# Who makes the lower weight parts in the recurrence stage: VectorE or GpSimd

## What is computed

```
q, k, v, xr, yr = split(rms_norm(x) @ w_in)
attn_out = attention(q, k, v)
xc = depthwise_conv(xr)                       # 4 taps
r, i = sigmoid(xc @ wa + ba), sigmoid(xc @ wx + bx)
a = exp(8 * r * log_sigmoid(lam));  b = sqrt(1 - a*a) * i * xc
h_t = a_t * h_(t-1) + b_t                     # forward, and once more backward
lru_out = (h_fwd + h_bwd) * gelu(yr)
x = x + concat(attn_out, lru_out) @ w_out     # the first output projection
```

## Time and profile before

| | us |
|---|---|
| median of 3 runs (3453.57 to 3456.44) | 3454.61 |
| the profiled execution, its own time | 3458.81 |
| its span in the trace | 3457.0 |
| TensorE busy in the span | 3363.4 (97%) |
| VectorE, ScalarE, GpSimd busy | 2208.1, 1435.4, 1123.1 |

### The profile page before, as it was taken

The page is one execution under the profiler, slowest core; times in us unless marked ns, Lnnn a source line. Parts: engine busy times, 40 slices in busy tenths (PEclk is TensorE's granted clock), DMA queues, the critical chain, the costliest instruction groups (busy, mean ns, idle before and its releaser), DMA issues.

```text
span 3457.0 us, 44808 instructions
## 1 busy us (share of the span) xinstructions
PE 3363.4 (97%) x16634; PEld 2711.7 (78%) x16634; DVE 2208.1 (64%) x2247; ACT 1435.4 (42%) x1901; POOL 1123.1 (32%) x644
## 2 busy tenths in 40 slices
PE   9999899999999999999999999999889999999998
PEld 6677777888888868888887777777667878888886
DVE  8996968777773474322277888888856564444434
ACT  5688835444441142333223443344453353333213
POOL 2000028888832212111111111111112376766222
PEclk9999999999999999999999999999999999999999
DMA  4210221222252112111111110111122212223322
GB/s 143 62 44 19 73 90 67 81 85 79 85 195 95 48 43 92 36 42 36 37 49 43 37 42 31 42 42 36 43 79 85 79 63 90 76 88 122 134 89 82
DMA packets 59167, 242.52 MB, mean 70 GB/s; under 512 B 6592, under 2 KB 6592, under 8 KB 53312
## 3 DMA queue, kind: packets, MB, share of 16 engines
q1 hardware_dynamic: 59072, 241.22, 19.7%
HBM read 194.53 MB, written 41.42 MB: 68 GB/s over the span
## 4 chain that ended last, share of the span: by engine, by line
PE 81%; DVE 13%; issue 3%; ACT 3%; DMA 0%; POOL 0%; DVEq 0%; POOLq 0%; ACTq 0%
PE ps L508 45%; PE ps L1459 24%; PE ps L2699 2%; PE ps L2711 2%; PE ps L2688 1%; PE ps L2849 1%; PE ps L2862 1%; DVE conv_acc L2312 1%; DVE t_wide L1096 1%; PE ps L531 1%; PE ps L2801 1%; PE ps L2856 1%; PE ps L2835 1%; DVE small L2352 1%; PE ps L2797 1%
## 5 line engine op out<-in xcount | busy, mean ns | idle before, releaser
L479 POOL TENSOR_TENSOR w_lo_part<-w_raw,w_hi_part 128x1024 fp32r<-128x1024 f32 x162 | 404.7, 2498 | 1736.3 <-ACT w_hi_part L462 1736.3
L508 PE MATMUL ps<-h_hi_part,w_hi_part 128*128 128x512 f32 x1904 | 623.5, 408 | 30.1 <-DVE h_lo_part L1632 12.0
L508 PE MATMUL ps<-h_lo_part,w_hi_part 128*128 128x512 f32 x1904 | 594.7, 393 | 0.0
L508 PE MATMUL ps<-h_hi_part,w_lo_part 128*128 128x512 f32 x1904 | 593.1, 392 | 0.0
L462 ACT ACTIVATE w_hi_part<-w_raw 128x1024 fp32r<-128x1024 f32 x180 | 189.1, 1051 | 719.5 <-PE ps L508 631.7
L508 PEld LDWEIGHTS ps<-h_hi_part,w_hi_part 128*128 128x128 f32 x1904 | 346.4, 190 | 126.0 <-issue 41.6
L508 PEld LDWEIGHTS ps<-h_hi_part,w_lo_part 128*128 128x128 f32 x1904 | 360.5, 189 | 78.2
L508 PEld LDWEIGHTS ps<-h_lo_part,w_hi_part 128*128 128x128 f32 x1904 | 360.6, 189 | 78.0 <-issue 0.3
L2312 DVE SCALAR_TENSOR_TENSOR conv_acc<-u_pad,cols,conv_acc 128x1024 f32<-128x1024 f32 x232 | 307.3, 1325 | 19.4 <-DVE conv_acc L2312 2.7
L2151 DVE TENSOR_TENSOR residual<-residual,ps 128x1024 f32<-128x1024 f32 (+1 forms) x60 | 73.2, 1220 | 268.0 <-PE ps L508 267.9
L508 PE MATMUL ps<-u_hi,w_hi_part 128*128 128x512 f32 x736 | 232.0, 390 | 0.0
(11 more groups left out here) (449 smaller groups left out, 6596.8 us busy)
## 6 DMA issues: line engine op xcount, KB each, us to landing
w_raw<-in_w SPq DMA_DIRECT2D x226, 512.0 KB, 3.3
w_raw_odd<-in_w SPq DMA_DIRECT2D x46, 512.0 KB, 3.8
u_spill<-ffn_u SPq DMA_DIRECT2D x46, 512.0 KB, 3.0
u_wide<-u_spill SPq DMA_DIRECT2D x23, 1024.0 KB, 9.1
residual<-in_x SPq DMA_DIRECT2D x4, 1024.0 KB, 10.5
both_halves<-q_chan SPq DMA_DIRECT2D x16, 256.0 KB, 4.4
x_again<-in_x SPq DMA_DIRECT2D x8, 512.0 KB, 3.9
residual<-in_x SPq DMA_DIRECT2D x2, 2048.0 KB, 7.2
```

What stands on the lines that cost most here:

```text
L479: pool.tensor_tensor(WLO[:, slot], WRAW[:, slot], f32(WHI[:, slot]), ALU.subtract).then_inc(w_ready, 1)
L508: last = pe.matmul(PS[:, ps, b * HALF:(b + 1) * HALF], st[:, slot, k, :], at(mv, k, b), start=(k == 0 and n == 0), stop=(k == nk - 1 and n ...
```

## The change

The lower parts of jobs 9 to 19 are made by GpSimd, in the order of the jobs, each as soon as its upper part is there. VectorE no longer makes them; of this stage only job 20's stays with it. The arithmetic is the same.

```diff
@@ gpsimd_program
             splits_pool(pool, 0, J_GATE[0] + 1)
-            split_rest(pool, J_GATE[0] + 1)
+            for j in range(J_GATE[0] + 1, J_OUT + 2):
+                split_rest(pool, j)
             pool.wait_ge(w_ready, J_OUT + 2)
@@ vector_program
             def conv(t):
-                split_rest(dve, J_GATE[t])
                 dve.wait_ge(xc_tap, t + 1)
...
                 st.do(dve.tensor_tensor_scan(y[:, way], p[:, way], i[:, way], 0.0, ALU.mult, ALU.add))
-                if d == 0:
-                    split_rest(dve, J_YR[t] + 2)
-
-            dve.wait_ge(w_ready, J_GATE[0] + 2)
+
             for t in range(4):
                 inputs(t)
-                split_rest(dve, J_GATE[t] + 2)
                 if t < 3:
                     conv(t + 1)
```

## The result

The changed kernel takes 3462.37 us (median of 21 runs, 3460.01 to 3465.94), the kernel before, in as many runs beside it, 3458.41. The ratio is 1.0014, with a 95% interval of 1.0008 to 1.0020: the change makes the kernel slower, by 4.0 us or 0.11% by the medians. The profiled execution took 3464.93 with a span of 3462.8; that of before, 3458.81 and 3457.0.

The account below looks back on a forecast made before the run. VectorE's row from first tap to last product was taken as the bound: 112.0 less 12.1 removed plus 16.4 of holds gives 116.3, +4.3 us, so 3454.61 + 4.3 = 3458.9 us; 8-in-10 range 3454 to 3463.

Parts of the forecast that it names:

- VectorE's row as the bound: First tap (326.18) to last product (end 438.15): VectorE's nearly unbroken work, 112.0 us, sets when everything behind starts.
- What is removed, 12.1: VectorE's stretch: nine subtractions of jobs 11 to 19 and three gaps go, 12.1 us, leaving 99.9 of 112.0.
- the three gaps: VectorE's waits of 1.17 ahead of job 14, 1.14 ahead of a scan, 0.41 ahead of taps; counted as gone.
- The hold, 7 x 2.08 + 2 x 0.9 = 16.4: GpSimd's subtractions delay VectorE's two-operand instructions: seven full tiles at 2.08, two halves at 0.9, 16.4 us added.
- the row at 452.43: VectorE instruction with one PSUM operand, 1.21 with GpSimd at work from 452.74; taken to show PSUM readers are not held.
- No hold: Rival: VectorE's plain f32 instructions run beside GpSimd; TensorE's pace limits the gain to -5.8, 3448.8 us; chance 0.05.
- Little change: Rival: GpSimd begins ahead of VectorE's instruction in gaps left, 1.06 per full tile; -2.9, 3451.7 us; chance 0.08.
- Full hold: Rival: GpSimd blocks VectorE for its whole printed instruction, 2.41 full, 1.2 half; +7.2, 3461.8 us; chance 0.17.
- what the sum means: +4.3 us (0.12%) set against 0.2%, 6.9 us, as what a measurement can tell; 0.81 on within it.
- The absolute time: Median forecast for the changed kernel: 3454.61 + 4.3 = 3458.9 us.
- Whatever moves the end moves everything behind it by the same amount: Behind VectorE's last product: residual load, clearing, addition and TensorE's next job at 448.03 all shift equally, 4.3 us later.

Follow-up runs that it names:

- the spare reads: Kernel before, plus eleven unneeded 128x512 subtractions on GpSimd, VectorE still making the lower parts: 3465.98 against 3457.49, ratio 1.0027.
- writes alone: Kernel before, plus eleven GpSimd memsets of 128x512 at the same upper parts, no operand read: 3458.37 against 3457.49, ratio 1.0003.
- version with the halves beside the taps: Changed kernel, GpSimd's half tiles of jobs 13 and 16 also waiting for inputs(t) to end: 3463.51 against 3457.49, again 3461.87 against 3458.27.
- the version that removed them without GpSimd: Kernel before, VectorE making jobs 12, 15 and 18 ahead of inputs(t): 3455.62 against 3457.49, again 3456.86 against 3458.27.
- the version with GpSimd only where it costs nothing: Changed kernel, GpSimd keeping jobs 8, 9, 10, 13, 16, last two beside taps; VectorE makes 12, 15, 18 early: 3454.20 against 3458.27, again 3454.66 against 3458.37.

## Why the prediction was right and where it was wrong

**VectorE's row as the bound: right.** The stretch follows VectorE's instructions, holds and gaps in the changed kernel and the six others, and each came out within 0.5 us of its expectation but for the spare reads (2.6 off). The medians go with it as far as they can tell, with intervals of 2 to 4 us to either side: stretches of 108.1, 109.1, 111.8, 112.0 (writes alone), 116.2 and 120.6 have times of -4.1 (again -3.7), -1.9 (again -1.4), +0.9, +0.9, +4.0 (again +4.4) and +8.5 us against before. The version with the halves beside the taps (114.2; +6.0 and +3.6) is the one that doesn't fit. From the end of the stretch to TensorE's next start, 9.8 to 10.3 us pass in every kernel, so the link to that start holds as well.

**What is removed, 12.1: right.** The nine subtractions are gone and so are the three gaps. That the gaps were late weights and not something else is shown by the version that removed them without GpSimd.

**The hold, 7 x 2.08 + 2 x 0.9 = 16.4: right.** Measured on the full tiles: L2511 3.24, 3.22 and 3.23 (2.01 more on the mean), the scans 4.38, 4.37 and 4.37 (2.08 more), L2523 3.20 (1.97 more); on the halves 3.46 - 2.48 = 0.98 twice. The sum is 3 x 2.01 + 3 x 2.08 + 1.97 + 2 x 0.98 = 16.2. They stand where the prediction put them, but for job 19, of which it named the direction alone. 112.0 - 12.1 + 16.2 = 116.1, and 116.2 was measured. Two small things were off without a part in the sum: GpSimd's rows are printed up to 4.20 long, not 3.4, and the row at 452.43 could not show that an instruction that reads PSUM is free, since VectorE had begun it before GpSimd; the taps beside the moved halves show it (3.92).

**The rivals.** *No hold* fell by these rows and by the spare reads. *Little change*, where GpSimd begins first and costs 1.06, fell too: VectorE has no idle time in the row, so GpSimd never began first. At 344.98 it waited 0.43 for L2523's end, was printed 2.70, and the scan paid in full. *Full hold* fell by its size: GpSimd's printed 2.4 hold VectorE for 2.0 to 2.1. The sentence of the Trainium skill on which it stood (SBUF — State Buffer, section "Who interferes with whom") is right that the two exclude each other; the runs here show 0.3 to 0.4 us less of it than the 2.41 that GpSimd's undisturbed row prints. The price goes by GpSimd's tile and not by VectorE's instruction: one that takes 1.22 and a scan of 2.29 pay the same 2.0 to 2.1.

**The step that failed: what the sum means.** Every case of mine of any weight had a sign, and the sum's was +4.3 us; I put 0.81 on no difference because I set 0.2%, 6.9 us, as what a measurement can tell. The forecast's own range (3456.5 to 3461 on 3454.61; by 1.8 per tile its lower end would be 3456.9) lay wholly above the kernel before, by 1.9 us at least. The bound was never worked out from rows: the three runs shown for before lie within 2.9 us of each other, and medians of that spread over some twenty runs tell far less than 6.9. The measured interval is 0.08% to 0.20%, so 0.06% to either side, a third of what I set, and 4.0 us is a difference. With that bound at 0.1%, the same sum gives a forecast of slower.

**The absolute time** was off by 3.5 us, 3462.37 for 3458.9, and all of it comes from the base: the 3454.61 of three runs was 3458.41 in 21, 3.8 more, while the step was 0.3 smaller than forecast.

**"Whatever moves the end moves everything behind it by the same amount": only as far as TensorE's next start.** At the second half's addition the shift is 450.93 - 446.66 = 4.27, of which 3.9 come from the end of VectorE's row and 0.4 from the passage behind it. Two things act there and behind that the prediction did not have. First, TensorE's clock. These are the windows of TensorE (stretch, its length, TensorE's busy time and instructions, granted clock, DMA share, GB/s), first of after, then of before:

```profile
444.50:450.00 5.50, 5.47 (x12) 0.51 0.72 310
450.00:452.30 2.30, 0.00 (x1) 1.00 0.56 173
452.30:456.00 3.70, 3.70 (x11) 0.63 0.10 39
```
```profile
440.60:443.60 3.00, 2.98 (x12) 1.00 0.98 421
443.60:448.00 4.40, 0.03 (x1) 0.88 0.58 212
448.00:452.00 4.00, 3.97 (x9) 0.50 0.01 4
```

And these are the first of the twelve products in TensorE's timeline, again of after and of before:

```profile
444.48 1.22 PE L508 MATMUL ps<-h_hi_part,w_hi_part 128*128 128x512 f32 x2 [3.56 <-DVE h_lo_part L1633]
```
```profile
440.62 0.73 PE L508 MATMUL ps<-h_hi_part,w_hi_part 128*128 128x512 f32 x2 [1.81 <-DVE h_lo_part L1632]
```

The same twelve products follow a wait of 1.81 before and run at a granted 1.00 (2.4 GHz), in 3.0 us; after, they follow a wait of 3.56 and run at 0.51, so at about 1.2 GHz, in 5.5. That is why they, and not the residual's load, are last in the chain: job 20's upper part waits for them. The length of the wait alone does not tell the clock. In the two executions of the version with GpSimd only where it costs nothing, the same products follow waits of 1.77 and 1.80, and the first pair takes 0.73 in one and 1.07 in the other. The next wait is then shorter, 2.33 against 4.40, and the 240 products behind it take 56.28 where they took 57.40, so 1.1 comes back. At their end the shift is 508.58 - 505.43 = 3.15.

Second, what comes far behind. The two profiled executions of the changed kernel start the 240 products within 0.03 us of each other and yet need 56.28 and 54.70 for them. The rows are the chain of the first and of the second, and then of before; the 144 products are a place far behind the stage that the chains of all kernels have.

```profile
452.30 56.28 PE ps L508 x240
...
1289.81 32.64 PE ps L508 x144
```
```profile
452.33 54.70 PE ps L508 x240
...
1287.79 32.64 PE ps L508 x144
```
```profile
1286.18 32.64 PE ps L508 x144
```

Against before, the two are 4.27 and 4.30 late at the start of the 240 products, 3.63 and 1.61 at the 144, and 5.8 and 3.6 by their spans (3462.8 and 3460.6 against 3457.0). So single executions lose and regain some 2 us far behind the stage, and the medians are the better number. That theirs is 4.0, so close to the 4.3 of the sum, is in part luck: no rows show those 4.3 us carried through to the end.

**What became of the 2 us of the halves.** TensorE starts the 240 products 2.3 us earlier than in the changed kernel (449.98 against 452.30 and 452.33). These are the chain's rows of the version with the halves beside the taps:

```profile
449.98 56.28 PE ps L508 x240
...
1288.99 32.64 PE ps L508 x144
```

From the end of the 240 products to the start of the 144 it takes 782.7 us, in its second profile too. The changed kernel takes 781.2 and 780.8, before 780.8, and the seven other profiles 780.3 to 780.8. So 1.5 to 2.0 us of its gain are lost there, in both its profiles: that is shown. At the 144 it is 0.8 ahead of the first profile of the changed kernel and 1.2 behind the second. The first feed-forward pair lies in between, and these of TensorE's waits from 500 to 1290 differ, first of the version with the halves beside the taps, then of the changed kernel (its second profile):

```profile
PE ps L1462 <- ACT copy_x L1166: 2.5, 1, 2.5
PE ps L1462 <- DVE ps L1340: 2.1, 1, 2.1
PE ps L1462 <- DVE t_lo L1095: 1.0, 2, 0.7
PE ps L1462 <- DVE ffn_val L1348: 0.9, 1, 0.9
```
```profile
PE ps L1460 <- DVE ps L1338: 4.3, 1, 4.3
PE ps L1460 <- DVE t_lo L1093: 0.3, 1, 0.3
```

The changed kernel waits once for 4.3 there, and its products behind that run slowly at first (granted 0.62 and 0.69 from 545 to 550 and from 550 to 555). The other waits 2.1, runs on at a granted 1.00, and then waits 4.4 more in four places. Why its waits fall otherwise after a shift of some 2 us, no run was made to isolate; it stays open.

## What to carry to other kernels

Where VectorE's row of two-input SBUF instructions sets the end of a stage, work handed to an idle GpSimd is not free: each full-tile subtraction that fell on such an instruction cost VectorE 2.0 to 2.1 us here, where VectorE does the tile itself in 1.15. Hand over only what falls beside VectorE's PSUM reads or idle time, and look at late operands first: three subtractions made one step earlier took 2.9 us off the stretch with no work handed over (1.9 and 1.4 by the medians, within the noise). And work out what a measurement can tell from the spread of the runs before calling a signed sum "no change".

## What was not expected of the hardware

- In a row without idle time the price of the hold is nearly the same wherever GpSimd is released: 1.94 to 2.09 over all runs, whether it waited 0.4 for a VectorE instruction to end or 2.2. For half a tile it is 0.93 to 1.12. GpSimd's row is printed longer by its wait (2.70, 4.20, 4.42), so its length is no price.
- A tensor_tensor_scan over two SBUF inputs is held like a plain subtraction (4.38 for 2.29), and holds GpSimd.
- The same twelve products took 3.0 us before, behind a wait of 1.81, and 5.5 in the changed kernel, behind one of 3.56, at granted clocks of 1.00 and 0.51. In this way an engine that waits, and is no bound, came onto the chain; but waits of 1.77 and 1.80 in two executions of one kernel were followed by a fast and a slow first pair (0.73 and 1.07).
